# Key rows fetched and used inside the choice of experts

## What is computed

```python
q = (h @ w_pq).reshape(B, S, PEER_HEADS, 2, half)           # 8 heads
s1 = einsum('bshd,hnd->bshn', q[..., 0, :], sub_keys[0])    # 128 scores each
s2 = einsum('bshd,hnd->bshn', q[..., 1, :], sub_keys[1])
v1, i1 = lax.top_k(s1, 16)
v2, i2 = lax.top_k(s2, 16)
cand = v1[..., :, None] + v2[..., None, :]                  # 16 x 16 sums
top, pos = lax.top_k(cand, 16)
idx = take_along_axis(i1 * 128 + i2, pos)                   # 16 experts a head
gates = softmax(top)
act = gelu(einsum('btd,bthkd->bthk', h, peer_u[idx]))       # key rows
out = einsum('bthk,bthkd->btd', gates * act, peer_v[idx])   # value rows
```

## Time and profile before

| | us |
|---|---|
| median of 3 runs | 3617.41 (3610.5 to 3620.65) |
| the profiled execution, its time | 3627.49 |
| its span, first to last instruction | 3625.4 |
| TensorE busy in it | 2841.6 (78%) |
| VectorE busy | 2470.3 (68%) |
| ScalarE busy | 1025.6 (28%) |
| GpSimd busy | 968.2 (27%) |

### The profile page before, as it was taken

One profiled execution on the slowest core, in us unless ns is written; L12 is line 12 of the kernel. 1 busy time (PEld: TensorE's weight loads), 2 busy tenths in 40 slices (PEclk: granted clock), 3 DMA queues, 4 the chain that ended last, 5 costly groups with the idle time before them and its releaser, 6 DMA issues. The chain is left out here.

```text
span 3625.4 us, 41905 instructions
## 1 busy us (share of the span) xinstructions
PE 2841.6 (78%) x15588; PEld 2205.8 (61%) x15588; DVE 2470.3 (68%) x3846; ACT 1025.6 (28%) x1461; POOL 968.2 (27%) x1028
## 2 busy tenths in 40 slices
PE   5888769947399667888769921555699999999999
PEld 4667448626287226687268420111597898997797
DVE  3656776687877786645976788788655655657654
ACT  2533220010200013433110010011254554545653
POOL 0000044564554561000054567777200000000000
PEclk8988779979699868988689955776799999999999
DMA  6664799999999995653999999999654455554253
GB/s 243 219 245 148 283 386 423 422 407 413 346 395 422 405 380 188 234 189 105 370 377 423 420 393 407 420 397 390 232 180 163 160 178 179 169 179 134 71 185 128
DMA packets 225445, 1033.96 MB, mean 285 GB/s; under 512 B 29256, under 2 KB 32408, under 8 KB 167192
## 3 DMA queue, kind: packets, MB, share of 16 engines
q1 hardware_dynamic: 77848, 495.17, 37.3%
q0 software_dynamic: 147456, 536.94, 37.2%
HBM read 1030.96 MB, written 1.05 MB: 285 GB/s over the span
## 5 line engine op out<-in xcount | busy, mean ns | idle before, releaser
L276 DVE TENSOR_TENSOR w_lo<-raw,w_hi 128x1024 fp32r<-128x1024 f32 (+1 forms) x460 | 551.7, 1205 | 531.0 <-ACT w_hi L263 530.1
L1994 POOL DMA_INDIRECT arena_layer<-in_peer_u,arena_layer x512 | 481.4, 940 | 1304.8 <-SPq L922 929.8
L2060 DVE CUSTOM_DVE_ANT_0 arena_layer<-arena_layer,ps 128x1024 f32<-128x1024 f32 x512 | 608.5, 1219 | 155.4 <-DMA arena_layer<-in_peer_u,arena_layer 147.9
L698 PE MATMUL ps<-hT_hi,w_hi 128*128 128x256 f32 x2240 | 643.2, 287 | 37.7 <-PEq L1199 16.1
L263 ACT ACTIVATE w_hi<-raw 128x1024 fp32r<-128x1024 f32 (+1 forms) x460 | 478.6, 1044 | 678.2 <-PE ps L698 675.9
L2056 DVE SCALAR_TENSOR_TENSOR ps<-arena_layer,ps 128x1024 f32<-128x1024 f32 x428 | 551.5, 1289 | 143.0 <-DMA arena_layer<-in_peer_v,arena_layer 118.0
L698 PE MATMUL ps<-hT_lo,w_hi 128*128 128x256 f32 x2240 | 641.8, 286 | 0.0
L698 PE MATMUL ps<-hT_hi,w_lo 128*128 128x256 f32 x2240 | 641.4, 286 | 0.0
L698 PE MATMUL ps<-parts_context,raw 128*128 128x256 f32 x2496 | 547.0, 383 | 56.4 <-PEq L922 56.4
L1994 POOL DMA_INDIRECT arena_layer<-in_peer_v,arena_layer x512 | 486.7, 950 | 294.6 <-DVE ps L2056 172.8
L698 PEld LDWEIGHTS ps<-parts_context,raw 128*128 128x128 f32 x2496 | 479.2, 192 | 124.0 <-issue 57.8
(11 more groups left out here) (389 smaller groups left out, 2803.1 us busy)
## 6 DMA issues: line engine op xcount, KB each, us to landing
raw<-in_ffn_w_gu SPq DMA_DIRECT2D x154, 1024.0 KB
raw<-in_w_mod SPq DMA_DIRECT2D x72, 1024.0 KB
raw<-in_ffn_w_down SPq DMA_DIRECT2D x70, 1024.0 KB
raw<-in_w_ada SPq DMA_DIRECT2D x48, 1024.0 KB
raw<-in_w_in SPq DMA_DIRECT2D x44, 1024.0 KB
raw<-in_conv_w_in SPq DMA_DIRECT2D x24, 1024.0 KB
raw<-in_w_o SPq DMA_DIRECT2D x8, 1024.0 KB
raw<-in_w_pq SPq DMA_DIRECT2D x8, 1024.0 KB
```

Of the source, the lines that this page charges most:

```text
L276: dve.tensor_tensor(self.lo[:, k, 0:n], self.raw_part(g, t, parity, k // 2, g.starts(t, k), g.starts(t, k + 1)), self.hi[:, k, 0:n].bitcas ...
L698: mm = pe.matmul(out_, stay, move, start=start and n == 0, stop=stop and n == len(combos) - 1, skip_group_check=True)
L1994: gp.indirect_dma_start(self.grow[:, slot % GR, :], None, self.tables[slot // half_way], bass.IndirectOffsetOnAxis(ap=self.index[:, k:k + ...
L2060: dve.tensor_tensor_reduce(row, row, self.tile, 1.0, 0.0, ALU.mult, ALU.add, cell).then_inc(row_used.sem, 1)
```

## The change

1. The ring and the choice no longer share memory: `sc`, `eq` and `cand` move to the tensor `parts` (which is allocated for the context path before the choice now), so the ring `grow` is free during the choice.
2. Pool gets a program in the choice: it waits for tile 0's `index` (semaphore `index_made`), then fetches 1 head (layer 0) or 2 (layer 1) and the 8 slots ahead.
3. VectorE takes those rows in tile 1's part: 2 rows behind each pair of candidate searches, 4 behind each of the six long lookup operations, until all 16 or 32 are used.
4. In layer 0 the `down` of z00 takes 2 heads for 3; in layer 1 `alone` is left with 2 heads for 4.

```diff
-    def peer_select(l, sc, best, bestf, cand, pos, p12, eq, sel, index, gate):
+    BESIDE_SEARCH, BESIDE_LOOKUP = 2, 4
+
+    def peer_select(l, sc, best, bestf, cand, pos, p12, eq, sel, index, gate, experts, heads):
...
+            @block.gpsimd
+            def _(gp):
+                gp.wait_ge(index_made.sem, index_made.at(1))
+                experts.fetch(gp, heads)
...
+                def rows_beside(t, n):
+                    for slot in range(taken[0], min(taken[0] + n * t, heads * TOPK)):
+                        experts.use(dve, slot // TOPK, slot % TOPK, slot % TOPK + 1)
+                        taken[0] = slot + 1
...
                     for h in range(0, PEER_HEADS, 2):
                         top16_pair(dve, v, *[
                             (top[:, k, :], pos[:, k, :], cand[:, k, 0:CANDS]) for k in (h, h + 1)])
+                        rows_beside(t, BESIDE_SEARCH)
...
                         v.link(dve.tensor_tensor(e4, sel[:, k].unsqueeze(3).to_broadcast(shape),
                                                  steps16, ALU.is_equal))
+                        rows_beside(t, BESIDE_LOOKUP)
                         v.link(dve.tensor_tensor(e4, e4, bf[:, :, k, :].unsqueeze(2).to_broadcast(shape),
                                                  ALU.mult))
+                        rows_beside(t, BESIDE_LOOKUP)
                         v.link(dve.tensor_reduce(sel[:, k], e4, AX_X, ALU.add))
+                        rows_beside(t, BESIDE_LOOKUP)
...
+                    dve.scalar_tensor_tensor(out=index[:, t], in0=sel[:, 0], scalar=float(NKEYS),
+                                             in1=sel[:, 1], op0=ALU.mult, op1=ALU.add) \
+                       .then_inc(index_made.sem, 1)
...
-        sc = rest[:, 4096:8192].rearrange("p (t half n) -> p t half n", t=TT, half=2)
+        begin_parts(f"context_{l}", 2048 + D_FF * TT, F32)
+        sc, eq, cand = carve((TT, 2, 1024), (PEER_HEADS, 256), (PEER_HEADS, CANDS), of=parts)
...
+        peer_select(l, sc, best, bestf, cand, pos, p12, eq, sel, index, gate, experts, 1 + l)
         if l == 0:
-            context_ffn("z00", 0, 0, 0, experts, (1, 5, 3, 1))
+            context_ffn("z00", 0, 0, 0, experts, (1, 5, 2, 1))
```

More of the change, by code:

```diff
@@ L438, in _build @@
     acts_weighed = signal("acts_weighed")
+    index_made = signal("index_made")
     cols_ready = signal("cols_ready")
@@ L1860, in _ @@
                 v = Steps(dve, vec_step)
+                taken = [0]
+                def rows_beside(t, n):
+                    for slot in range(taken[0], min(taken[0] + n * t, heads * TOPK)):
+                        experts.use(dve, slot // TOPK, slot % TOPK, slot % TOPK + 1)
+                        taken[0] = slot + 1
                 for t in range(TT):
@@ L1901, in _ @@
                                                  steps16, ALU.is_equal))
+                        rows_beside(t, BESIDE_LOOKUP)
                         v.link(dve.tensor_tensor(e4, e4, bf[:, :, k, :].unsqueeze(2).to_broadcast(shape),
                                                  ALU.mult))
+                        rows_beside(t, BESIDE_LOOKUP)
                         v.link(dve.tensor_reduce(sel[:, k], e4, AX_X, ALU.add))
+                        rows_beside(t, BESIDE_LOOKUP)
                     v.link(dve.tensor_scalar(sel[:, 1], sel[:, 1], float(l * NKEYS * NKEYS), None,
                                              ALU.add))
-                    v.link(dve.scalar_tensor_tensor(out=index[:, t], in0=sel[:, 0],
-                                                    scalar=float(NKEYS), in1=sel[:, 1],
-                                                    op0=ALU.mult, op1=ALU.add))
+                    dve.scalar_tensor_tensor(out=index[:, t], in0=sel[:, 0], scalar=float(NKEYS),
+                                             in1=sel[:, 1], op0=ALU.mult, op1=ALU.add) \
+                       .then_inc(index_made.sem, 1)
                     v.link(dve.tensor_copy(stat[:, 0:8], top[:, :, 0]))
@@ L1925, in _ @@
                                          ALU.add))
+        experts.end_phase(heads)
+        index_made.base += TT
         vec_ready.base += TT
@@ L3602, in _build @@
         pos, p12 = pos.bitcast(U32), p12.bitcast(U32)
-        cand = rest[:, 0:2048].rearrange("p (h n) -> p h n", h=PEER_HEADS)
-        eq = rest[:, 2048:4096].rearrange("p (h n) -> p h n", h=PEER_HEADS)
+        grow = rest[:, 0:GR * D].rearrange("p (r n) -> p r n", r=GR)
+        acts = rest[:, GR * D:GR * D + 256]
+        flat_index = index.rearrange("p t h k -> p (t h k)")
         with nc.Block(no_gpsimd_drain=True) as block:
```

## The result

The changed kernel takes 3631.43 us (median of 8 runs, 3622.35 to 3638.07) against 3619.68 us of the kernel before (8 runs). That is 11.8 us more by the medians; the ratio of the two is put at 1.0036, 95% interval 1.0023 to 1.0048, or 13 us. The forecast was +7.2 us, 3624.6, with a range of 3608 to 3641. The profiled execution's span is 3636.0 us, 10.6 more than before.

A forecast was written before the change was run, and what follows sets the result against it. VectorE was taken to end both choices of experts, TensorE `down`. Layer 0 +12.2 us (24 - 7.3 - 1.5 - 3) and layer 1 -5 gave +7.2, so 3624.6 us, with a range of 3608 to 3641.

The forecast's parts named there:

- Layer 0's choice, +24: Layer 0's choice of experts: 20.0 us of exposed VectorE work plus 4.1 us waiting for rows; bounds +20 and +35.
- The weight stream: Layer 0's choice: slowed to two thirds, w_mod lasts to 497; the exponential is ready at 502.7, before VectorE comes at 507.
- Norm, -7.3: Norm stage behind layer 0's choice: finds its rows in a full ring, 21.3 us in place of 28.6.
- `down`, -1.5: Layer 0's `down` loses a head, TensorE's 76.6 us stay; only VectorE's 4.1 us tail shrinks (0 to -4.1).
- Add, -3: Add stage behind layer 0's `down`: its rows came late by 1.83 and 1.14 us; now the ring is full.
- Layer 1: Choice +42 us (38.7 to 50), norm -7, stage of rows alone -40 for two fewer heads; sum -5.
- The carry-over to the median: Whole kernel: +7.2 us on the profiled execution carries over to the runs' median, 3617.4 + 7.2 = 3624.6.
- Rival B: Rows come too slowly to the searches, 5 us each, with waits between tile 1's lookups; +22 us, 3639; chance 0.20.
- C: DMA engines are the one bound, so moved rows cost nothing and idle DMA time is gained; -18 us, 3599; chance 0.10.
- D: The gathers' issues hold VectorE's searches in both choices; +20 us, 3645; chance 0.06.
- E: Rows land only after the weight stream, so the searches' rows are in effect serial; near no change, 3617; chance 0.06.
- The two rules: DMA split beside weights: a third for gathers, against equal shares (row every 2.5 us); exclusive SBUF lock: trace shows only Pool held.

The follow-up runs named there:

- e1: The changed kernel with the change kept in layer 0 only, layer 1 as in the kernel before; 3633.62 us, ratio 1.0036 to the kernel before.
- e3: The changed kernel with the choice's rows used in one piece behind tile 1's index, not between searches and lookups; 3627.58 us, ratio 1.0016 to the kernel before.
- e8: The changed kernel, timing only: row products in the choice read 128 of 1024 columns; 3723.19 us on a slower chip, ratio 0.9983 to the kernel before.
- the kernel before again: The kernel before, rerun unchanged as a yardstick on a third chip; 3618.91 us, ratio 0.9999.
- e9: Against the kernel before: layer 0 gathers only the ring, from tile 1's index; layer 1 uses two heads behind tile 1's index; 3611.97 us, ratio 0.9981.
- second group: Four variants of the changed kernel run on one slower chip, where the kernel before takes 3726.91 us; the variants took 3720.02 to 3723.33 us.
- e5: The changed kernel with layer 0's head taken from the norm stage, not from `down`; 3722.24 us on a slower chip, ratio 0.9995 to the kernel before.

## Why the prediction was right, and where its sizes were off

- **The mechanism** (the head was hidden in `down` and isn't in the choice): right. `down` 76.6 to 75.7 us with 25.4 us of idle VectorE behind the rows; e1 puts the whole loss into layer 0.
- **Layer 0's choice, +24**: measured +28.6. The step that failed is "land from 436 on every 3.72 us". The pace was right (3.71), the start wasn't: the first row landed at 443.8, 8.1 us after its issue ended (435.7), where the forecast had 4 (436 + 3.72 = 439.7). The rest of the 5 us by which the 16th was late (500.4 for 495.5) is one gap of 4.7 instead of 3.7, between the 6th and the 7th landing (462.4 and 467.1 by the view of transfers). e3 shows the same delay: 8.0 us from the end of the 9th gather's issue to its landing. And e8 shows that the landing alone sets the stage's end in layer 0, so those 5 us came through almost whole.
- **The weight stream** (last half at 497, columns at 502.7, wait for the exponential covered): measured 494.4, 500.0, covered by 11.9 us.
- **Norm, -7.3**: -6.8. **`down`, -1.5**: -2.8 (694.05 to 772.51, against 671.64 to 752.86). **Add, -3**: -3.2 (772.51 to 796.53, against 752.86 to 780.10). Small errors with the right signs. Layer 0 in sum, +12.2: A says +16.1.
- **Layer 1**: +42, -7, -40 forecast; +42.6, -6.8, -39.3 measured in the choice, the norm and the rows alone; -5 in sum against -2.0 by B. Half of the 3 us are in these three stages, which sum to -3.5 (the waits were 4.5 us, I had 3); the other 1.5 lie in stages that no edit touches, and are within B's spread.
- **The signs**: the choices end at 513.3 and 1875.5 (509 and 1870 forecast), the first gathers are issued at 434.6 and 1782.7; the 1765 given for the latter left out the shift by layer 0.
- **The carry-over to the median**: the two profiled executions differ by 10.6 us though the stages give 15.3 up to 2252.84. The kernel before took 1387.9 us from there to its end, the changed one 1383.2, and the kernel before again 1382.7. So these 4.7 us belong to that one execution of the kernel before. The stages say +14.1 (A and B), twice the forecast of +7.2; that the medians came out nearer to it, at +11.8, is no merit of the prediction.
- **Rival B**: by the prediction's own sign (waits for `in_peer_u` well above 4 and 3 us) the 8.8 and 4.5 us point to B. Its cause, a pace slower than 3.72, is not what happened; its place, the waits between tile 1's lookups, is where the missing 5 us lie. Its price is also not worked out: at one row per 5 us throughout, 436 + 16 x 5 = 516 is 20 us past 495.5, not 11. **C** is refuted by `down` (DMA share 0.96 in the changed kernel, TensorE still 75.7 us) and by e1. **D** is refuted in its size: the lookups take 2.29 us beside a held issue, and the one operation that is held costs 0.17 us a layer (next point). **E** is refuted by the rows used from 460 on.
- **The two rules.** Rows came at a third of the DMA engines' rate beside the weight stream. The prediction set this against the rule of equal turns between queue rows, a packet at a time (the Trainium skill, "DMA: Bandwidth & Descriptors", Queues, rings and completion order). It read equal turns as equal shares, and that step was wrong: the trace agrees with the rule. From 446 to 498 us, both queues full, the two sent as many packets each (packets, MB, share of the engines; q1 has the weights, q0 the gathers):

```profile
q1 hardware_dynamic: 2009, 14.62, 66.7%
q0 software_dynamic: 2037, 7.39, 35.0%
```

A weight packet holds twice the bytes of a row's packet (14.62 / 2009 = 7.3 KB and 7.39 / 2037 = 3.6 KB on average), so turns are equal and bytes are two to one. Of the exclusive lock (the Trainium skill, "SBUF — State Buffer", section "SBUF: two separate sides") the runs show mostly one direction: GpSimd's issue, begun behind VectorE's product of two SBUF tiles, is held: the longest in the choices takes 2.86 us (layer 1, 1859.46), an undisturbed one 0.94. The other direction shows once a layer and is small: the cast that precedes the lookups falls into an issue, ends with it, and takes 0.40 us for 0.23 before. A lookup that began inside an issue (1852.34) kept its 2.29 us.

```profile
477.05 0.94 POOL L2015 DMA_INDIRECT arena_layer<-in_peer_u,arena_layer  x1 [0.30 <-DVE arena_layer L2081]
...
477.64 0.40 DVE L1904 CAST y_tok<-y_tok 128x128 f32<-128x128 uint32 x1
```

## What to carry to other kernels

Work that stands beside another engine's unbroken run costs little there, whatever its own length; before moving it, look at how long its engine stands idle once it is gone, for that is what the new place has to beat. A transfer that is started early beside a full stream should be timed by its first landing and not by its pace alone, and its share of the stream by the size of its packets. And a move that bundles two things, here a prefetch of the ring and a head of work, should be tried apart: in layer 1 the prefetch gained 5 to 7 us and the heads nothing; in layer 0 the head lost, and the prefetch gained 2.6 us only when it began behind the stream.

## What the runs showed of the hardware

A gather issued while nothing else was queued had landed and was in use 3.8 us after its issue ended (486.86 to 490.63, before), and 4.2 us after it in e9, where the last weight half was still landing; behind a weight stream that keeps all 16 engines busy it took 8.1 us (changed kernel) and 8.0 (e3), though rows then followed every 3.7 us. Two queues that are both full took turns packet by packet (2009 and 2037 packets in 52 us), so their bytes went by packet size.

On the second group's chip the kernels took 3720 to 3727 us instead of 3611 to 3634. Its traces show TensorE idle without any releaser, as in the conv projection of e5 (waits: total, times, longest):

```profile
PE ps L699 <- issue: 27.8, 26, 2.0
```

The changed kernel's own trace has no such wait there. VectorE shows the like ahead of small operations, 0.3 to 1.9 us each in the choices. What holds the engines up there wasn't found; for that reason the readings above take from that chip only layer 0's choice, norm, `down` and add, and neither gate-up nor what stands behind it.
